# Early sequences' value pages in the prompt's attention stage, and sigmoid gates written with tanh

## What is computed

```
r_past = reverse_cumsum(logf_past) - logf_past                  # per key and head
s = [ (q . k_past) * scale + r_past ,  (q . k_new) * scale - a_new ]   # 4096 old keys and the new one (+ a_new in all)
p = softmax(s);   o_fox = p_past @ v_past + p_new @ v_new       # v_past: 32 pages of 128 x 512 a sequence
```

```
br_k   = o_k * silu(gate_k)                                     # k: the three branches
merged = sum_k sigmoid(bgate_k) * (br_k @ w_branch_k)           # 1024 wide
y      = x + rmsnorm(merged @ w_out, g_post)                    # eps 1e-6
```

## Time and profile before

| | |
|---|---|
| time, median of 3 runs | 1461.28 us (1459.33 to 1465.89) |
| the profiled execution | 1460.96 us, span 1459.2 us, mean granted clock of PE 0.892 |
| PE busy | 1209.6 us (83%) |
| DVE busy | 801.3 us (55%) |
| ACT busy | 240.1 us (16%) |
| moved by DMA | 282 MB, mean 193 GB/s |
| value pages of the forgetting branch | 256 loads of 256 KB, 512 matmuls of L1614, 80.0 us busy |

### The profile page before, as it was taken

The page is one execution under the profiler, slowest core; times in us unless marked ns, Lnnn a source line. Parts: engine busy times, 40 slices in busy tenths (PEclk is TensorE's granted clock), DMA queues, the critical chain, the costliest instruction groups (busy, mean ns, idle before and its releaser), DMA issues. The chain is left out here.

```text
span 1459.2 us, 27607 instructions
## 1 busy us (share of the span) xinstructions
PE 1209.6 (83%) x10095; PEld 824.0 (56%) x10095; DVE 801.3 (55%) x1186; ACT 240.1 (16%) x681; POOL 173.7 (12%) x149
## 2 busy tenths in 40 slices
PE   0755677999999687998878998989796979798995
PEld 0755566886887474555556875546463645454241
DVE  1344340398999833456672457485857586725023
ACT  0000041112111201334451110100101010100113
POOL 0000000110000000000004031405050505040000
PEclk9968878999999765889999999989998999998898
DMA  8898504277888715100008449798978788676740
GB/s 224 243 305 245 198 31 145 88 240 231 282 268 300 198 23 203 44 1 1 1 1 262 136 143 324 232 304 259 318 233 278 239 296 275 229 235 212 265 190 30
DMA packets 205702, 282.01 MB, mean 193 GB/s; under 512 B 21614, under 2 KB 126599, under 8 KB 205119
## 3 DMA queue, kind: packets, MB, share of 16 engines
q1 hardware_dynamic: 109758, 202.40, 41.4%
q10 hardware_dynamic: 89376, 60.01, 14.3%
q0 software_dynamic: 6432, 17.83, 3.8%
HBM read 273.26 MB, written 11.11 MB: 195 GB/s over the span
## 5 line engine op out<-in xcount | busy, mean ns | idle before, releaser
L1581 PE MATMUL bank<-xnT,e_wg 128*128 128x260 f32 x1152 | 280.8, 402 | 0.5 <-DMA e_wg<-in_w_in 0.5
L1581 PEld LDWEIGHTS bank<-xnT,e_wg 128*128 128x128 f32 x1152 | 227.3, 200 | 76.5 <-issue 28.5
L585 PE MATMUL score_banks<-xnT,oT 128*128 128x260 f32 (+1 forms) x864 | 198.2, 388 | 9.9 <-DMA oT<-in_w_in 9.9
L1565 POOL DMA_INDIRECT d_slc<-in_cache_nsa_slc,selrow x128 | 154.5, 1207 | 380.2 <-PE score_banks L1652 336.1
L585 PEld LDWEIGHTS score_banks<-xnT,oT 128*128 128x128 f32 (+1 forms) x864 | 162.3, 190 | 40.3 <-DMA oT<-in_w_in 10.1
L249 PE MATMUL score_banks<-c_cols,c_w 64*64 64x64 f32 (+1 forms) x4096 | 96.5, 253 | 96.0 <-issue 57.0
L249 PEld LDWEIGHTS score_banks<-c_cols,c_w 64*64 64x64 f32 x4096 | 91.6, 166 | 100.7 <-issue 100.7
L1589 PE MATMUL bank<-oT,e_wb 128*128 128x512 f32 x192 | 101.1, 676 | 23.3 <-DVE cst L1843 11.8
L299 DVE COPY c_cols<-oT 128x1024 f32<-128x1024 f32 x48 | 48.9, 1146 | 101.2 <-DMA oT<-in_cache_nsa_cmp 82.0
L1614 PE MATMUL bank<-d_vpage,d_pf 128*8 128x512 f32 x512 | 80.0, 637 | 20.5 <-DMA d_vpage<-in_cache_fox_kv 20.5
L1589 PEld LDWEIGHTS bank<-oT,e_wb 128*128 128x128 f32 x192 | 40.0, 216 | 82.8 <-issue 82.6
(11 more groups left out here) (367 smaller groups left out, 1430.5 us busy)
## 6 DMA issues: line engine op xcount, KB each, us to landing
d_vpage<-in_cache_fox_kv SPq DMA_DIRECT2D x256, 256.0 KB, 4.7
d_kpage<-in_cache_fox_kv SPq DMA_DIRECT2D x96, 256.0 KB, 5.2
oT<-in_cache_fox_kv SPq DMA_DIRECT2D x80, 256.0 KB, 4.0
mt<-in_cache_fox_kv SPq DMA_DIRECT2D x80, 256.0 KB, 3.7
e_wg<-in_w_in ACTq DMA_DIRECT2D x36, 512.0 KB, 6.0
oT<-in_cache_nsa_cmp SPq DMA_DIRECT2D x128, 128.0 KB, 3.8
oT<-in_w_in ACTq DMA_DIRECT2D x13, 1024.0 KB, 7.9
oT<-in_cache_nsa_cmp ACTq DMA_DIRECT2D x64, 128.0 KB, 3.6
```

Of the source, the lines that this page charges most:

```text
L585: last = nc.tensor.matmul(pj[ch.n % 2][i][0:ch.w, 0:NM if ch.mem else TH], w[:, c, ch.off:ch.off + ch.w], rhs, start=c == 0, stop=c == DC - 1)
L1565: nc.gpsimd.indirect_dma_start(out=slc[:, n, :], out_offset=None, in_=k.cache_slc, in_offset=bass.IndirectOffsetOnAxis(ap=k.selrow[:, at:a ...
L1581: last = nc.tensor.matmul(gate_bank[n % 2][:, 0:TH], wg[product % WR][:, c, :], k.xnT[:, c, part * TH:(part + 1) * TH], start=c == 0, stop ...
```

## The change

Four things change.

1. In `middle`, the softmax of the five early sequences over the forgetting branch is done for all five at once, on 1280 columns: the sum with `rpast`, maximum over pages, transpose, maximum, spread over the partitions by a product with ones, subtraction, exponential, sum, reciprocal, product. The hidden products are cut in three pieces to make room for the two small PE products. Some small operations are moved ahead.
2. In `prompt`, SP loads the 160 value pages of these sequences, four of them in a batch, through a ring of four pairs of pages. PE multiplies a group of four pages in each of the units 4 to 47, eight groups a sequence, and after them `fold` turns the sums (45 entries, one per unit). The outputs are written between the loads, one behind every third batch, so the window state stands behind batch 29 of 0 to 39. The PSUM bank is taken from the attention's results, which now have one bank for both groups, and the probabilities' buffers shrink to three key tiles, so that units of four key tiles are copied in two pieces.
3. In `sample_and_merge` only the sequences 5 to 7 keep the forgetting branch. Their page scores move one step ahead (steps 0 to 5), their softmax is in steps 2, 4 and 6, their value groups in steps 3 to 7 (4, 4, 4, 4 and 8), and nothing of it is left in the tail; other steps' softmax has 20 columns. w_out is loaded in two halves.
4. The branch gates are tanh(x/2) instead of sigmoid(x); VectorE's product takes (tanh + 1) * z, and so `merged` is doubled, which 4 * EPS in the norm makes good.

```diff
--- before.py
+++ after.py
@@ middle: exponentials, the hidden products in three pieces @@
+        sc.wait_ge(x_shifted, 1)
+        nc.scalar.activation(k.sfe[:, :, :, :], k.sfe[:, :, :, :], ACT.Exp).then_inc(x_exp, 1)
+        sc.wait_ge(x_shifted, 2)
+        nc.scalar.activation(fnew, fnew, ACT.Exp).then_inc(x_exp, 1)
...
-        hidden(3)
+        hidden(3, 0, 8)
+        te.wait_ge(x_max, 1)
+        te.wait_ge(grow_done, 2)
+        nc.tensor.transpose(fox_max, fmx[:, :, :].rearrange("p b h -> p (b h)"), k.ident).then_inc(x_turned, 1)
+        hidden(3, 8, 12)
+        te.wait_ge(x_dia, 1)
+        nc.tensor.matmul(fox_spread, k.ones[0:EH, :], fdia[:, :], start=True, stop=True).then_inc(x_spread, 1)
+        hidden(3, 12)
...
+        te.wait_ge(x_den, 1)
+        nc.tensor.matmul(fox_den, k.ones, fden[:, :, :].rearrange("p b h -> p (b h)"), start=True, stop=True).then_inc(x_spread_den, 1)
@@ middle: VectorE @@
+        nc.vector.tensor_tensor(early, early, k.rpast[:, 0:EARLY * PAGES, :].rearrange("p (b n) h -> p b n h", b=EARLY), ALU.add).then_inc(x_scored, 1)
...
+        ve.wait_ge(x_scored, 1)
+        nc.vector.tensor_reduce(fmx[:, :, :], by_head, AX, ALU.max).then_inc(x_part, 1)
...
+        ve.wait_ge(x_new, 1)
+        ve.wait_ge(x_part, 1)
+        nc.vector.tensor_tensor(fmx[:, :, :], fmx[:, :, :], fnew, ALU.max).then_inc(x_max, 1)
+        ve.wait_ge(x_turned, 1)
+        nc.vector.tensor_reduce(fcol[:, :], fox_max, AX, ALU.max).then_inc(x_col, 1)
+        ve.wait_ge(x_col, 1)
+        nc.vector.tensor_scalar(fdia[:, :], k.ident[0:EH, 0:EH], fcol[:, 0:1], None, ALU.mult).then_inc(x_dia, 1)
+        ve.wait_ge(x_spread, 1)
+        nc.vector.tensor_tensor(early, early, over_pages(fox_spread), ALU.subtract).then_inc(x_shifted, 1)
+        nc.vector.tensor_tensor(fnew, fnew, fox_spread.rearrange("p (b h) -> p b h", b=EARLY), ALU.subtract).then_inc(x_shifted, 1)
...
+        ve.wait_ge(x_exp, 2)
+        nc.vector.tensor_reduce(fden[:, :, :], by_head, AX, ALU.add).then_inc(x_part, 1)
+        ve.wait_ge(x_part, 2)
+        nc.vector.tensor_tensor(fden[:, :, :], fden[:, :, :], fnew, ALU.add).then_inc(x_den, 1)
...
+        ve.wait_ge(x_spread_den, 1)
+        nc.vector.reciprocal(frd[:, :, :].rearrange("p b h -> p (b h)"), fox_den).then_inc(x_rden, 1)
+        ve.wait_ge(x_rden, 1)
+        nc.vector.tensor_tensor(early, early, frd[:, :, :].unsqueeze(2).to_broadcast([P, EARLY, PAGES, H]), ALU.mult).then_inc(x_done, 1)
+        nc.vector.tensor_tensor(fnew, fnew, frd[:, :, :], ALU.mult).then_inc(x_done, 1)
@@ prompt: buffers and the order of entries @@
-pt = [sb("f_pt", [P, 2, NT, T]), k.mt[:, :, :].rearrange("p (j t) n -> p j t n", j=2)]
-nm, su = (sb("f_" + n, [P, U, 2]) for n in ("nm", "su"))
+pt = [sb(f"f_pt{i}", [P, 2, 3, T]) for i in range(2)]
+KV, VG = 2, 4
+QUAD = PAGES // 4
+work = [(b, g) for b in range(EARLY) for g in range(QUAD + 1)]
+work_of = {u + 4: at for u, at in enumerate(work)}
-pt_bank, o_bank = ps[4:6], ps[6:8]
+pt_bank, o_bank, fv_bank = ps[4:6], ps[6], ps[7]
@@ prompt: SyncE @@
-        for dst, src in outs:
+        left = list(outs)
+        for at in range(0, EARLY * PAGES, 2 * KV):
+            _, pages = nc.values_load_multi_w_load_instructions(k.table[0:1, at:at + 2 * KV], engines=[sp.engine], min_val=0, max_val=POOL - 1)
+            for i, pg in enumerate(pages):
+                n = (at + i) // KV
+                if i % KV == 0 and n >= VG:
+                    sp.wait_ge(v_free, n - VG + 1)
+                sp.dma_start(vpage[:, (n % VG) * KV + i % KV, :].unsqueeze(1),
+                             k.cache_fox[bass.ds(pg, 1), :, 1, :].rearrange("a p n -> p a n")).then_inc(v_in[n % VG], 16)
+            if at // (2 * KV) % 3 == 2 and left:
+                sp.dma_start(*left.pop(0)).then_inc(out_done, 16)
+        for dst, src in left:
             sp.dma_start(dst, src).then_inc(out_done, 16)
@@ prompt: TensorE @@
+        def page_values(b, g):
+
+            if g == 0:
+                te.wait_ge(fv_zero, 1)
+                after(te, sums_placed, 2 * b)
+            for i in range(4):
+                n, page = (b * PAGES + 4 * g + i) // KV, 4 * g + i
+                if i % KV == 0:
+                    te.wait_ge(v_in[n % VG], 16 * KV * (n // VG + 1))
+                last = nc.tensor.matmul(fv_bank[32 * i:32 * i + H, :], k.sfe[:, b, page, :], vpage[:, (n % VG) * KV + i % KV, :],
+                                        start=g == 0, stop=g == QUAD - 1, skip_group_check=True)
+                if i % KV == KV - 1:
+                    last.then_inc(v_free, 1)
+                if page == 0:
+                    nc.tensor.matmul(fv_bank[0:H, :], k.snew[0:NB, 0, b, :], k.srow[:, M_FV:M_FV + BRW], start=False, stop=False,
+                                     skip_group_check=True)
+
+        def fold(b):
+            te.wait_ge(sums_out, b + 1)
+            for c in range(4):
+                last = nc.tensor.matmul(of_turned[:, 2 * c:2 * c + 2], fvs[:, c // 2, (c % 2) * P:(c % 2 + 1) * P], k.fold[:, 2 * c:2 * c + 2],
+                                        start=True, stop=True, skip_group_check=True)
+            last.then_inc(folded, 1)
...
+            if u.no in work_of:
+                b, g = work_of[u.no]
+                if g < QUAD:
+                    page_values(b, g)
+                else:
+                    fold(b)
             turn(u)
@@ prompt: VectorE's and ScalarE's copies of the turned probabilities (turned_parts: the fourth key tile by itself) @@
-            nc.vector.tensor_copy(transposed(u, 0), in_bank(u, 0)).then_inc(pt_left, 1)
+            for dst, src in turned_parts(u, 0):
+                last = nc.vector.tensor_copy(dst, src)
+            last.then_inc(pt_left, 1)
...
+        def page_sums(b):
+            sc.wait_ge(v_free, (b + 1) * PAGES // KV)
+            after(sc, folded, b)
+            nc.scalar.activation(fvs, fv_bank[:, :].rearrange("p (a n) -> p a n", a=2), ACT.Copy).then_inc(sums_out, 1)
+
+        def place_sums(b):
+            sc.wait_ge(folded, b + 1)
+            for j in range(2):
+                rows = slice(64 * j, 64 * j + 64)
+                nc.scalar.activation(k.of[rows, :, b:b + 1], of_turned[rows, :].rearrange("p (c j) -> p c j", j=2)[:, :, j:j + 1],
+                                     ACT.Copy).then_inc(sums_placed, 1)
@@ sample_and_merge: where the late sequences' pages go @@
-first_step = lambda b: 1 + (b - EARLY) * GROUPS // PER
+first_step = lambda b: (b - EARLY) * GROUPS // PER
+fox_of = {first_step(b) + 2: b for b in range(EARLY, NB)}
+fox_no = lambda b: fox_of[b] - EARLY
+values_at = {}
+for b in fox_of:
+    if b + 2 < NB:
+        values_at[b + 1] = (fox_no(b), 0, GROUPS // 2)
+        values_at[b + 2] = (fox_no(b), GROUPS // 2, GROUPS)
+    else:
+        values_at[b + 1] = (fox_no(b), 0, GROUPS)
+sums_after = {b: f for b, (f, _, end) in values_at.items() if end == GROUPS}
+stats = lambda b: 4 if b in fox_of else 3
+stats_until = lambda b: sum(stats(i) for i in range(b + 1))
+heads_of = lambda b: NS if b in fox_of else NS - H
-groups_of = lambda b: range((b - 1) * PER, b * PER) if 1 <= b <= LATE // PER else range(0)
+groups_of = lambda b: range(b * PER, (b + 1) * PER) if b < LATE // PER else range(0)
@@ sample_and_merge: SyncE @@
...
+        keys, values = KG, 0
+        for b in range(NB):
+            if b:
+                load_small(b)
+            if b * PER == LATE:
+                sp.wait_ge(k_free, LATE)
+                sp.dma_start(wout[:, 0:4, :], k.w_out[0:D // 2].rearrange("(c p) n -> p c n", p=P)).then_inc(wout_in, 16)
+            keys_end = min((b + 1) * PER + KG, LATE)
+            values_end = values
+            if b in values_at or b + 1 in values_at:
+                f, _, end = values_at.get(b, (0, 0, 0))
+                values_end = min(f * GROUPS + end + VG, LATE)
+            for which in (0, 0, 1, 0, 1, 1, 0, 1, 1, 1, 1, 1):
+                if which == 0 and keys < keys_end:
+                    load_pages(sp, 0, keys)
+                    keys += 1
+                if which == 1 and values < values_end:
+                    load_pages(sp, 1, values)
+                    values += 1
+        sp.dma_start(wout[:, 4:DC, :], k.w_out[D // 2:D].rearrange("(c p) n -> p c n", p=P)).then_inc(wout_in, 16)
@@ sample_and_merge: TensorE's step @@
+            if b - 1 in sums_after:
+                turn_fox(sums_after[b - 1], b - 2)
...
+            f, first, end = values_at.get(b, (0, 0, 0))
             for i in range(4):
-                if b:
-                    page_values(b - 1, i, i + 1)
+                if end:
+                    page_values(f, first + i, first + i + 1)
                 merge_until(b, 2 + i)
-            if b:
-                page_values(b - 1, 4, 6)
+            if first + 4 < end:
+                page_values(f, 4, 6)
             merge_until(b, 6)
             softmax_step(b, 0)
-            if b:
-                page_values(b - 1, 6, 7)
```

(43 more changed lines are left out.)

208 lines of the change are left out of this document (119 added, 89 removed).

## The result

The changed kernel takes 1477.04 us (median; 1467.88 to 1482.48) against 1459.33 us of the kernel before in the same runs: a ratio of 1.0104, 95% interval 1.0078 to 1.013, some 15 us slower. The profiled execution has a span of 1471.5 us (before 1459.2) at a mean granted clock of 0.897.

The account below looks back on a forecast made before the run. PE was taken to bound prompt, and the loop's steps to be set partly by PE, partly by VectorE's chain. Middle 4.5, prompt +63.6, loop -31.3, tail -19 sum to +17.8, so 1479 us; own range 1469 to 1500, whole 1449 to 1505.

Parts of the forecast that it names:

- Products in the forgetting units: Prompt stage: 11 page groups and 2 row products at half clock add 22.7 us (12.6 to 36).
- R1: Rival, chance 0.15: page products keep prompt's forgetting units at 2.4 GHz, a set 18 us, the whole 1455.
- Products in the other units: Prompt's later sets: 33.4 us of groups, row products and folds, less 13 filling idle PE, +20.4 (17 to 28).
- The feed: Prompt stage: SP's loading of 42 MB of value pages lags a little behind PE, +3 us (0 to 12).
- the 2-MB output: Prompt stage: pages behind this write in SP's queue wait for it, +1.5 us.
- R4: Rival, chance 0.10: pages come late at each prompt unit, PE stands and the clock falls, +25, 1504 us.
- The state copy: Prompt stage: pages behind the 4088-KB window-state copy in SP's queue wait for it, 15 plus 1 us for the clock.
- R2: Rival, chance 0.13: the window-state copy holds back nothing in prompt, half of the engines being free; 1462 us.
- The loop: Sample loop: less page, softmax and key-score work in the steps, -31 us in sum (bounds -24 and -42).
- Tail: After the loop: eight page groups go and the late x_prompt comes earlier, -19 us (-15 to -21).
- Middle: Middle stage: subtraction, exponential and sum of the added softmax stay in line, +4.5 us (2.5 to 9).
- Gates: Branch gates: three-operand products cost nothing and table loads may go, 0 us taken (ends 0 and -16.7).

## Why the prediction came out right

**Sum and sign** were right, 1479 against 1477.04, but the sum was partly luck. In prompt the forgetting units were put 17 us too high (22.7 against 5.7) and the later eight sets 21 too low (20.4, 3 and 17.5 together against 61.8), and these two nearly cancel in +63.6 against +68.6. In the loop, too, wrong terms add up right.

**Products in the forgetting units**, +22.7: wrong. The step "at half clock 11 x 1.89 + 2 x 0.97" took the clock of the kernel before. Sets 1 to 3 grew by 1.0, -0.9 and 5.6, 5.7 in all, under even the low end of 12.6. By the prediction's own sign, a clock over 0.9, R1 is what happened in this place, though its 18 us a set were 21.49 and 19.60; the runs with narrow products and without loads show that the wide products did it. The row against R1, page products alone at 0.50 in the tail, doesn't carry over to products between other work. The rule of the Trainium skill (TensorE: Matmul & The Clock Gate, Part 1) beside which the rival stood, that sustained matmul work lifts the throttle, agrees with the sets at 1.00, and still not with that row, nor with the first set, where PE was busy throughout at 0.58. The high end of 36 doesn't follow from its rows: 22.7 + 20.5 - 13.96 is 29.2.

**Products in the other units**, +20.4: about right as a price. Without loads the eight sets are 129.5 us against 103.4, 26 more, some of it at the clock of the sets with folds (0.91).

**The feed**, +3, and the 2-MB output, +1.5: mis-sized. Seven groups waited 13.1 us for late pages, 4.5 of it behind that output, and the groups at the lower clock add 8.4. R4 was half of what happened: late pages in seven of 40 groups, not in each.

**The state copy**, 15 + 1: right in size (14.05 and a slow group, 16.0) and place (the seventh group of sequence 3, in unit 37). Its reason, "SP's queue is one", fits the packets of the changed kernel, which leave no gap for the pages behind them, but it is not the whole: from another queue the wait is 15.61. R2's argument, that half of the engines are free, is true of half of each page's packets, and a page needs all of them.

**The loop**, -31.3: right as a sum, wrong in its terms. "Two groups and the turning, 2.5 us in six steps" gives -15, but the pages alone, with the turning left in, gave 7.9 in all, 2.6 of it in the first parts. The softmax over 264 elements gave 9.9, where I had 3.3. The rest, 15.0, is a difference, and no run tried it alone. Of it 12.3 lies in the step that lost its key scores (54.52 against 66.83 with pages and softmax cut), so these are likely most of it; beyond the first part that step got 9.3 shorter than before, where I had 5. Step 0 took the key scores for 1.3. The 5.5 given to step 1 was 1.4, and the 4 given to step 7 was 0.9. The pages' going was worth less than their PE time, with a clock that fell as they went, 0.88 against 0.92, and a first part that waits for VectorE's softmax chain as much as for PE; what each of the two cost isn't shown. The bound of -42 is -44.6 by its own terms, if all of step 6 falls off.

**Tail** -19 against -21.2 from the last transpose, or 101.37 to 79.94 by the windows, -21.4: right in size; its terms weren't tried one by one, and the clock rose with it, from 0.88 to 0.94. **Middle** +4.5 against +1.65 in this pair; over the runs middle is 57.9 to 62.2 us in kernels without the change and 63.8 to 70.3 in those with it, so 4.5 is a fair price. **Gates** 0: right, as far as half a per cent can be told.

## What to carry to other kernels

Before a stage is given a stream of small awaited loads, look what long transfers are in flight there: here a copy in packets of 64 KB held up the loads that shared its engines, from their own queue and from another, and it belongs where nothing is awaited. PE work that was moved took the clock along, so its price at the new place and its worth at the old one can't be read from durations at the old clock. And a sum that comes out right says little of its terms until each has been left out by itself.

## What the runs showed of the hardware that was not expected

The same forgetting sets ran at a granted clock of 0.56 and 0.63 with page products of 2 columns between them, at 1.00 with products of 512 columns, and at 0.75 with none at all (0.91 and 0.75 in the trace without the early pages, where prompt is as before). A 4-MB copy on ScalarE's queue held up page loads of SP's queue for 15.61 us at a DMA share of 0.58: its packets of 65,408 bytes took 2.41 us each, with about the time of one page packet between two of them.
